# Row norms in a three-block transformer kernel: mean squares summed on ScalarE, row updates in halves of 512 columns, the feed-forward's residual taken chunk by chunk

## The reference, cut to what matters

```python
# block one
h = rms_norm(x, g_pre_mix) * (1 + sc1) + sh1
x = x + gt1 * rms_norm(hybrid_mixer(h), g_post_mix)
h = rms_norm(x, g_pre_ffn) * (1 + sc2) + sh2
x = x + gt2 * rms_norm(moe_ffn(h), g_post_ffn)
# block two, its last line (DEEPNORM_ALPHA = 2 ** 0.25)
x = layer_norm(DEEPNORM_ALPHA * x + ff(x), ln2_g, ln2_b)
# block three
u = modulate(rmsnorm(x, norm1), sh1, sc1)
x = x + g1 * token_mixer(u)
u = modulate(rmsnorm(x, norm2), sh2, sc2)
x = x + g2 * hier_moe(u)
return rmsnorm(x, final_norm)
```

## Time and profile before

| | us |
|---|---|
| median of three runs | 2443.75 |
| lowest and highest | 2442.85, 2445.37 |
| the profiled execution | 2448.2 |
| its span | 2446.3 |

### The profile page before, as it was taken

The page is one execution under the profiler, slowest core; times in us unless marked ns, Lnnn a source line. Parts: engine busy times, 40 slices in busy tenths (PEclk is TensorE's granted clock), DMA queues, the critical chain, the costliest instruction groups (busy, mean ns, idle before and its releaser), DMA issues.

```text
span 2446.3 us, 34558 instructions
## 1 busy us (share of the span) xinstructions
PE 2042.8 (84%) x14185; PEld 1136.4 (46%) x14186; DVE 492.8 (20%) x1075; ACT 363.5 (15%) x808; POOL 321.5 (13%) x149
## 2 busy tenths in 40 slices
PE   6996698668768866989869889999889899889778
PEld 4774222112212211323228666889874546455444
DVE  1044411011111100211120484010221302141111
ACT  1231111001101100111111333100011113210001
POOL 4100212222222222221220000000000000001211
PEclk9988799889989988999979988999989999989999
DMA  9666679999999799997983643555533344349994
GB/s 325 171 242 238 284 302 407 426 426 412 403 426 405 306 425 425 392 406 310 410 319 126 219 166 114 218 166 139 196 124 120 112 143 140 127 185 408 410 410 160
DMA packets 183321, 681.49 MB, mean 279 GB/s; under 512 B 15970, under 2 KB 57220, under 8 KB 150225
## 3 DMA queue, kind: packets, MB, share of 16 engines
q1 hardware_dynamic: 179200, 670.02, 70.2%
q0 software_dynamic: 4032, 10.40, 1.7%
q10 hardware_dynamic: 16, 0.02, 0.0%
HBM read 679.33 MB, written 1.06 MB: 278 GB/s over the span
## 4 chain that ended last, share of the span: by engine, by line
PE 64%; DMA 23%; DVE 7%; ACT 3%; SPq 2%; issue 1%; POOL 0%; DVEq 0%; ACTq 0%; POOLq 0%
PE ps L775 33%; PE ps L1156 9%; DMA spare<-in_b_mlp 8%; DMA scr<-in_w_mlp 7%; PE ps L1182 5%; DMA MOD<-in_w_mlp 4%; PE ps L1479 2%; PE ps L1193 2%; DMA HTY<-in_w 2%; PE ps L810 2%; PE ps L1160 1%; PE ps L1124 1%; PE ps L856 1%; PE ps L1516 1%; PE ps L1490 1%
## 5 line engine op out<-in xcount | busy, mean ns | idle before, releaser
L1156 PE MATMUL ps<-ring,scr 128*32 128x512 f32 x2208 | 294.4, 682 | 134.7 <-POOL ring L721 134.3
L775 PE MATMUL ps<-ring,HTY 128*128 128x512 f32 (+5 forms) x960 | 328.4, 503 | 3.7 <-ACT HTY L1563 3.7
L721 POOL COPY ring<-scr 128x4096 f32<-128x4096 f32 x62 | 224.0, 3617 | 777.4 <-DMA scr<-in_w_mlp 572.3
L775 PEld LDWEIGHTS ps<-ring,HTY 128*128 128x128 f32 x960 | 175.5, 191 | 153.4 <-issue 137.3
L775 PE MATMUL ps<-HTY,ring 128*128 128x256 f32 (+1 forms) x1072 | 236.4, 383 | 2.1 <-DMA ring<-in_w_ff 1.0
L1156 PEld LDWEIGHTS ps<-ring,scr 128*32 128x32 f32 x2208 | 73.2, 121 | 350.4 <-POOL ring L721 182.9
L775 PEld LDWEIGHTS ps<-HTY,ring 128*128 128x128 f32 (+1 forms) x1072 | 204.3, 191 | 32.9 <-ACT HTY L1563 2.8
L2393 DVE TENSOR_SCALAR spare<-ps 128x256 f32<-128x256 f32 x46 | 19.5, 425 | 680.8 <-PE ps L1160 680.7
L1563 ACT ACTIVATE scr<-ps 128x512 f32<-128x512 f32 (+7 forms) x117 | 58.4, 500 | 497.8 <-PE ps L775 399.9
L1156 PE MATMUL ps<-MOD,scr 128*32 128x512 f32 x736 | 95.2, 638 | 35.4 <-DMA spare<-in_b_mlp 25.7
L775 PE MATMUL ps<-ring,scr 128*128 128x128 f32 (+1 forms) x1040 | 121.6, 280 | 1.4 <-DVE scr L2502 1.4
(11 more groups left out here) (461 smaller groups left out, 1926.7 us busy)
## 6 DMA issues: line engine op xcount, KB each, us to landing
scr<-in_w_mlp SPq DMA_DIRECT2D x94, 2048.0 KB, 25.6
ring<-in_w_mlp SPq DMA_DIRECT2D x34, 2048.0 KB, 21.0
MOD<-in_w_mlp SPq DMA_DIRECT2D x32, 2048.0 KB, 24.2
HTY<-in_w_mlp SPq DMA_DIRECT2D x32, 2048.0 KB, 22.2
ring<-in_w_ada SPq DMA_DIRECT2D x23, 2048.0 KB, 9.3
ring<-in_w_in SPq DMA_DIRECT2D x20, 2048.0 KB, 7.9
ring<-in_w_ff SPq DMA_DIRECT2D x16, 2048.0 KB, 9.5
ring<-in_w SPq DMA_DIRECT2D x16, 2048.0 KB, 16.6
```

The lines of the kernel that those rows point to most:

```text
L721: pool.tensor_copy(m1_slabs[j], m1_arrivals[j]).then_inc(moved[j], 1)
L775: mm = pe.matmul(o, lhs(k), rhs(k), start=begin and k == 0, stop=end and k == nk - 1)
L1156: mm = pe.matmul(ps[C1 * c:C1 * (c + 1), 0, :], XG[:, 2 * j + i, :], m1_slabs[j][:, i, BANK * c:BANK * (c + 1)], start=j + i == 0, stop=False)
```

## The change

**At `out1`** ACT squares each product bank with a sum over the row (`Square`, scale 1/32, `accum_out`) before it copies it; DVE adds the two halves' sums and the epsilon. Then DVE updates `H` and `X` in halves of 512 columns. ACT squares the whole row of `X` (`root_of_tile`, waits for `norm_input`) and takes the root with the epsilon as bias (`norm_root`). DVE needs only the reciprocal, and modulates in halves; PE turns each half as it comes (`halves=True`), so that `h2_ready` and `u1_ready`, `u2_ready` now count to four, in SP's and POOL's waits too.

**At the end of block one's experts** PE signals each tile's sums apart. ACT runs a root on a constant after the loop, squares each tile straight from PSUM and takes its root. DVE multiplies straight from PSUM. `x1_ready` comes tile by tile, and PE's wait for block two's parameters stands behind `turn(X)`.

**At `ff2`** DVE adds each chunk to `X` and takes its `bn_stats` as it comes. After the last there are two `bn_aggr` over eight chunks and one root for both tiles; the layer norm of both tiles stands ahead of both modulations. ACT's root stands ahead of the copy of the first `ada3d` piece, and its two squares stand around the copies of `mod_row(10)` and `mod_row(11)`.

**At `out3`** the gated update runs in halves as each bank is copied out; the rest is as at `out1`. The `memset` of the epsilon moves to the kernel's start.

```diff
@@ PE @@
-            def turn(src, ready=None, tiles=range(NT)):
+            def turn(src, ready=None, tiles=range(NT), halves=False):
                 for a in tiles:
-                    if ready is not None:
+                    if ready is not None and not halves:
                         pe.wait_ge(ready, a + 1)
                     for half in range(2):
+                        if halves:
+                            pe.wait_ge(ready, 2 * a + half + 1)
...
-                mm.then_inc(m1["sum" if last else "scatter"], 1)
+                    if last:
+                        mm.then_inc(m1["sum"], 1)
+                if not last:
+                    mm.then_inc(m1["scatter"], 1)
...
-            pe.wait_ge(x1_ready, 1)
+            turn(X, x1_ready)
             pe.wait_ge(block2_params_landed, 96)
-            turn(X)
@@ ACT @@
+            def root_of_squares(src, scratch, a):
+                step(act.activation(scratch, src, ACT.Square, scale=1.0 / 32.0, accum_out=square_means[:, a:a + 1]))
+                act.activation(square_roots[:, a:a + 1], square_means[:, a:a + 1], ACT.Sqrt, bias=small_eps).then_inc(norm_root, 1)
+            def root_of_tile(a, scratch):
+                inputs[0] += 1
+                act.wait_ge(norm_input, inputs[0])
+                root_of_squares(X[:, a, :], scratch, a)
...
-            def wide_by_tile(dst, roots_of_tile):
+            def wide_by_tile(dst, scratch=None, normed=False):
                 for a in range(NT):
                     for i in range(2):
                         b = product()
+                        if normed:
+                            act.activation(scratch[:, BANK * i:BANK * (i + 1)], b, ACT.Square, scale=1.0 / 32.0, accum_out=squares_of_half[:, i:i + 1])
                         read(dst[:, a, BANK * i:BANK * (i + 1)], b)
-                    for _ in range(roots_of_tile):
+                    if normed:
                         root(1)
+                    if scratch is not None:
+                        root_of_tile(a, scratch)
...
-            act.wait_ge(m1["sum"], 1)
-            for a in range(NT):
-                act.activation(Y[:, a, :].rearrange("p (c n) -> p c n", c=2), ps[:, 4 + 2 * a:6 + 2 * a, :], ACT.Copy)\
-                    .then_inc(m1["sum_read"], 1)
-            root(2)
+            act.activation(square_roots[:, 0:1], small_eps, ACT.Sqrt)
+            for a in range(NT):
+                act.wait_ge(m1["sum"], a + 1)
+                root_of_squares(ps[:, 4 + 2 * a:6 + 2 * a, :], Y[:, a, :].rearrange("p (c n) -> p c n", c=2), a)
@@ DVE @@
+            def tile_root(a):
+                normed[0] += 1
+                dve.wait_ge(norm_root, normed[0])
+                step(dve.reciprocal(rstd[:, a:a + 1], square_roots[:, a:a + 1]))
+            def rms_modulate_tile(shift, scale, ready, a):
+                tile_root(a)
+                for i in range(2):
+                    step(dve.scalar_tensor_tensor(H[:, a, side(i)], X[:, a, side(i)], rstd[:, a:a + 1], MOD[:, scale, side(i)], ALU.mult, ALU.mult))
+                    tell(dve.tensor_tensor(H[:, a, side(i)], H[:, a, side(i)], MOD[:, shift, side(i)], ALU.add), ready, 2 * a + i + 1)
...
-            add_gated_norm(Y, 5, m1["sum_read"], NT)
-            dve.sem_inc(x1_ready, 1)
+            for a in range(NT):
+                tile_root(a)
+                step(dve.scalar_tensor_tensor(Y[:, a, :], ps[:, 4 + 2 * a:6 + 2 * a, :].rearrange("p b n -> p (b n)"), rstd[:, a:a + 1], MOD[:, 5, :],
+                                              ALU.mult, ALU.mult))
+                tell(dve.tensor_tensor(X[:, a, :], X[:, a, :], Y[:, a, :], ALU.add), x1_ready, a + 1)
...
+            for i in range(8):
+                dve.wait_ge(product_free, end["ff1"] + i + 1)
+                c = slice(P * i, P * (i + 1))
+                step(dve.scalar_tensor_tensor(X[:, :, c], X[:, :, c], 2.0 ** 0.25, H[:, :, c], ALU.mult, ALU.add))
+                for a in range(NT):
+                    step(dve.bn_stats(chunk_stats[:, a, i, :], X[:, a, c]))
...
+                for i in range(2):
+                    dve.wait_ge(product_free, end["out3"] - (2 * NT - 1 - 2 * a - i))
+                    step(dve.tensor_tensor(H[:, a, side(i)], H[:, a, side(i)], MOD[:, 2, side(i)], ALU.mult))
+                    step(dve.tensor_tensor(X[:, a, side(i)], X[:, a, side(i)], H[:, a, side(i)], ALU.add))
+                dve.sem_inc(norm_input, 1)
+                rms_modulate_tile(3, 4, u2_ready, a)
```

More of the change, by code:

```diff
@@ L2065, in add_gated_norm @@
[L2065 to L2073 removed]
+            normed = [0]
```

81 lines of the change are left out of this document (41 added, 40 removed).

## The result

The changed kernel takes 2423.19 us (median of 4 runs, 2420.93 to 2426.76), beside 2444.56 for the kernel before (4 runs, 2442.85 to 2448.98). The ratio is 0.9915, with a 95% interval of 0.9897 to 0.9933. The medians differ by 21.4 us; the prediction had 21.9 and a time of 2421.8.

What follows compares the result with a forecast made beforehand. PE holds 64% of the chain, transfers 23%, VectorE 7%; PE idles at four row norms. Savings of 2.2 + 2.5 + 9.8 + 7.4 = 21.9 us off the median 2443.75 give 2421.8 us, range 2417.5 to 2429.5.

Steps and rivals of the forecast that it cites:

- `out1`, 2.2: From the last copy at `out1` to PE's next product: 11.87 us instead of 14.09, so 2.2 us less.
- The term on the two copies: At `out1`, both copies out of PSUM come 0.79 us later, because each half is squared and its sum read first.
- `out3`, 2.5: From the last copy at `out3` to the next product: 8.74 us instead of 11.26, so 2.5 us less.
- `ff2`, 9.8: From the last chunk's copy at `ff2` to the `in3` product: 16.63 us instead of 26.47, so 9.8 less.
- I count the same slow start: Behind `ff2`, PE's clock was taken to have fallen as before, so the `in3` product starts equally slowly.
- The experts' end, 7.4: End of block one's experts: the next product starts at 1267.40 instead of 1274.77, so 7.4 us less.
- just in time: Block two's last parameter row, issued at 1261.39 and taking 5.2 us, lands at 1266.6, before the `in2` product at 1267.40.
- Savings last through the expert loop: Behind `out1`, the 2.2 us survive the expert loop, since its transfer queue runs dry and PE releases new slabs.
- The reciprocal held by a memset: Rival, 25%: at the experts' end POOL's memsets hold tile 1's reciprocal; saving 19.2 us, time 2424.5.
- The loop doesn't swallow `out1`'s gain: Denies a rival, 10%: the transfer-bound expert loop swallows `out1`'s gain; saving 19.7 us, time 2424.0.
- The squares from SBUF: Rival, 5%: squares from SBUF take twice as long, costing 1.2 us per tile at `out1` and `out3`; 2424.2 us.
- The loop's beat: Rival, 3%: earlier starts put more of POOL's 62 slab copies onto the path; twelve more cost 43 us, giving 2465.

Runs made afterwards that it cites:

- the two repeats: The changed kernel run again without any edit, twice: 2422.92 us (ratio 0.9917) and 2422.94 us (ratio 0.9912).
- both profiles of that kernel: Changed kernel with divided parameter wait, whole passes except each last tile's modulation, last tile's update halved at experts' end; run twice: 2418.46 and 2421.27 us.

## Why the prediction was right

**The sum.** 21.9 us were predicted; the medians differ by 21.4 (and by 22.3 and 22.0 in the two repeats), the places by 20.7 in the first profile and 21.8 in the other two. The steps, one by one:

- *`out1`, 2.2: measured 2.48.* The term on the two copies was too large. Reading the square's sum (0.19) lies under the end of the square and the start of the copy, where the prediction had the three one after another: VectorE starts 1.28 us after the half is in PSUM, not 1.49.
- *`out3`, 2.5: measured 2.49.* Durations of 0.75 and 0.69 for the halves held exactly.
- *`ff2`, 9.8: measured 9.58.* The 0.26 by which the place is longer is small gaps, nearly all of it in the four layer-norm passes (5.50 with the gaps around their signals, 5.26 predicted). What was wrong is "I count the same slow start": the clock comes back 5.8 us into the `in3` product, and not 3.3, and the start costs 1.2 us more (0.9 and 1.0 in the other two profiles). The medians are too coarse to show it.
- *The experts' end, 7.4: measured 6.2, and 7.3 in two other profiles.* The step that failed is "just in time": the last parameter row is issued at 1257.01 and takes 6.8 us, not the 5.2 of the earlier trace rows, and PE waited for it. With the wait divided, the place is 9.08 us by the prediction's count, where 9.3 was predicted. PE waiting behind `turn(X)` for the parameters is the one of the prediction's signs of being wrong that came.
- *Savings last through the expert loop:* shown by `out1` put back; the stretch behind it keeps its length.
- *The start from a run above the median:* the prediction took the places off the median, not off the profiled execution. That was right: of the surplus of 6.5 us in the first pair of profiles, 5.8 lie in the stretch where the clock makes the difference, and they didn't repeat.

**How much of the hit is luck.** The interval of the ratio allows 16 to 25 us. That the median came within 0.5 is in part luck: `out1` was 0.3 better than its sum, `ff2` 0.3 worse, the experts' end 0.1 to 1.2 worse, and the slower start behind `ff2` does not show in the medians. That each place but one came within 0.3 of its sum isn't.

**The rivals.** The reciprocal held by a memset did not occur in the changed kernel because it ended 0.02 us before the memset; moved into it, it wasn't held either. The loop doesn't swallow `out1`'s gain. The squares from SBUF cost 1.06, not twice 1.01. The loop's beat got no worse: 130.8 us of idle time against 134.3.

**What can't be told.** The places put back one by one cost 2.5, 6.2 to 7.6, 10.1 and 2.55 us, and these add up to the change in the places (20.7 to 21.8). By the ratios they cost 5.1 to 6.8, 5.9, 12.0 and 4.2, which is some 7 us more than the 21 in all; each ratio has an interval of 3 to 7 us to either side, and the ratio of the changed kernel, from which each is counted, one of 4 to 6, so this may be chance. Only for `out1`, run twice, did it repeat in direction.

## What to carry to other kernels

Where PE idles behind a row norm, count the chain of one tile from PSUM to PE's next product, and take statistics off VectorE: ScalarE's square with a sum under other work, or counts by chunks while the product still runs, brought nearly all of the gain here (together with the two copies, the table load and the second wait for both tiles that went from the experts' end; these were put back place by place, not one by one); halving the passes brought 0.6 us, and only the last tile's halves pay, since only there can PE start early. When such a place gets shorter, look at what was "just in time" behind it: a transfer of 24 KB took 5 to 7 us to land and gave part of the gain back. And compare places, not spans: two executions of one kernel differ by 5 us in a stretch that no edit touched, while the places repeat to 0.03 us, but for the one that waits for a transfer.

## What the runs showed of the hardware that I had not expected

- The granted clock of one and the same stretch was 0.74 in one execution and 0.52 in another of the same kernel; that stretch of 480 us differs by 5 us, as much as the three profiles of that kernel differ outside the places (4.3 to 4.8 us).
- After twelve transposes of 128 columns in one go of 2.83 us the clock was back 4 to 8 us earlier, counted from the product behind them, than after goes of four or eight, at two places and in both profiles of that kernel, for 2 to 3 us each. Whether it is the number or the density of the transposes wasn't tested.
- A `tensor_scalar` on 128x2 numbers took 1.64 us beside GpSimd's memsets, and ended when they did; reciprocal, `tensor_tensor` and aggregation took their usual 0.16 to 0.21 beside them.
